# Joined 512-column products in the MLP, earlier weight splits for the latents, and gated outputs transposed in three parts

## What is computed

```python
# first_block, layer 0: moba and fox heads; layer 1: differential and sliding-window (swa) heads
y = concat([ya * silu(ga), yb * silu(gb)]);   x = x + y @ w_out_ab
...
y = concat([yc * silu(gc), yd * silu(gd)]);   x = x + y @ w_out_cd
# second_block, per layer i: a mixer (latent attention "mla", then stick-breaking), cross attention, MLP
lat = h @ w_dkv
c_q  = rmsnorm_2(lat[..., :384], g_q)
c_kv = rmsnorm_2(lat[..., 384:640], g_kv)
k_pe = lat[..., 640:]
q = c_q @ w_uq;  kv = c_kv @ w_ukv           # per head: 192 and 256 columns
...
h = h + mem_cross_attn(...)
h = h + square(relu(rmsnorm_2(h) @ w_in)) @ w_out      # w_in: 1024 x 4096
```

## Time and profile before

| | |
|---|---|
| median of 3 runs | 1026.99 us (1026.68 to 1027.73) |
| the profiled execution's own time | 1027.6 us |
| its span in the trace | 1025.8 us |
| PE busy | 989.2 us (96% of the span) |
| DVE busy | 627.6 us (61%) |
| ACT busy | 548.2 us (53%) |
| mean granted clock of PE | 0.985 of full speed |

### The profile page before, as it was taken

The page is one execution under the profiler, slowest core; times in us unless marked ns, Lnnn a source line. Parts: engine busy times, 40 slices in busy tenths (PEclk is TensorE's granted clock), DMA queues, the critical chain, the costliest instruction groups (busy, mean ns, idle before and its releaser), DMA issues.

```text
span 1025.8 us, 15748 instructions
## 1 busy us (share of the span) xinstructions
PE 989.2 (96%) x6172; PEld 879.7 (86%) x6172; DVE 627.6 (61%) x1208; ACT 548.2 (53%) x1029; POOL 38.3 (4%) x83
## 2 busy tenths in 40 slices
PE   8899999999999979999999999999999999999997
PEld 7677778787787979887999999899988889999995
DVE  5867545486864476656765555557873658455554
ACT  6575564366684445545744434455673557444352
POOL 4011000001130000000000000000000000000000
PEclk9899989999999989999999999999999999999999
DMA  9776312565332434343556565666435435565551
GB/s 288 218 164 124 124 41 88 163 202 164 123 114 62 122 90 150 124 128 121 182 186 200 173 201 176 235 164 177 152 103 185 146 104 195 176 203 171 198 186 42
DMA packets 114167, 158.14 MB, mean 154 GB/s; under 512 B 13783, under 2 KB 55085, under 8 KB 114093
## 3 DMA queue, kind: packets, MB, share of 16 engines
q1 hardware_dynamic: 113656, 156.56, 49.4%
q10 hardware_dynamic: 436, 0.56, 0.2%
HBM read 156.06 MB, written 1.05 MB: 153 GB/s over the span
## 4 chain that ended last, share of the span: by engine, by line
PE 84%; DVE 6%; ACT 4%; issue 2%; SPq 1%; DMA 1%; DVEq 0%; ACTq 0%
PE bank L475 24%; PE bank L476 24%; PE bank L477 24%; PE bank L613 3%; DVE w_lo L1771 2%; PE bank L638 2%; PE bank L627 2%; PE bank L607 1%; PE bank L529 1%; DMA raw<-in_w_in_ab 1%; ACT xT_hi L1319 1%; SPq L2472 1%; DVE xT_lo L1828 1%; ACT pb L1438 1%; PE bank L592 1%
## 5 line engine op out<-in xcount | busy, mean ns | idle before, releaser
L1771 DVE TENSOR_TENSOR w_lo<-raw,w_hi 128x1024 fp32r<-128x1024 f32 (+2 forms) x292 | 336.2, 1195 | 179.2 <-ACT w_hi L1274 178.9
L1274 ACT CAST w_hi<-raw 128x1024 fp32r<-128x1024 f32 (+2 forms) x292 | 283.4, 1027 | 146.6 <-DMA raw<-in_mlp_w_in 74.2
L475 PE MATMUL bank<-xT_hi,w_hi 128*128 128x256 f32 x784 | 224.5, 286 | 3.0 <-DVE xT_lo L1828 2.0
L476 PE MATMUL bank<-xT_lo,w_hi 128*128 128x256 f32 x784 | 222.5, 284 | 0.0
L477 PE MATMUL bank<-xT_hi,w_lo 128*128 128x256 f32 x784 | 222.5, 284 | 0.0
L475 PE MATMUL bank<-w_hi,xT_hi 128*128 128x512 f32 (+1 forms) x432 | 161.8, 375 | 9.0 <-issue 4.0
L477 PE MATMUL bank<-w_hi,xT_lo 128*128 128x512 f32 (+1 forms) x432 | 157.9, 365 | 0.0
L476 PE MATMUL bank<-w_lo,xT_hi 128*128 128x512 f32 (+1 forms) x432 | 157.8, 365 | 0.0
L475 PEld LDWEIGHTS bank<-xT_hi,w_hi 128*128 128x128 f32 x784 | 151.0, 193 | 4.9 <-issue 3.1
L476 PEld LDWEIGHTS bank<-xT_lo,w_hi 128*128 128x128 f32 x784 | 151.0, 193 | 0.7
L477 PEld LDWEIGHTS bank<-xT_hi,w_lo 128*128 128x128 f32 x784 | 151.1, 193 | 0.0
(11 more groups left out here) (243 smaller groups left out, 1096.8 us busy)
## 6 DMA issues: line engine op xcount, KB each, us to landing
raw<-in_mlp_w_in SPq DMA_DIRECT2D x32, 1024.0 KB, 5.4
raw<-in_mlp_w_out SPq DMA_DIRECT2D x32, 1024.0 KB, 5.1
raw<-in_w_in_ab SPq DMA_DIRECT2D x13, 1024.0 KB, 9.3
raw<-in_w_in_cd SPq DMA_DIRECT2D x13, 1024.0 KB, 5.1
raw<-in_xa_w_kv SPq DMA_DIRECT2D x8, 1024.0 KB, 5.2
raw<-in_sb_w_qkv SPq DMA_DIRECT2D x16, 512.0 KB, 5.1
raw<-in_w_out_ab SPq DMA_DIRECT2D x4, 1024.0 KB, 5.2
raw<-in_w_out_cd SPq DMA_DIRECT2D x4, 1024.0 KB, 5.2
```

The costliest lines, as they stand in the source:

```text
L475: pe.matmul(o, wh, ih, start=start, stop=False, skip_group_check=True)
L476: pe.matmul(o, wh, il, start=False, stop=False, skip_group_check=True)
L1274: nc.scalar.copy(w_hi[:, u % SLOTS, a], raw[:, u % SLOTS, a]).then_inc(hi_ready, 1)
L1771: V.tensor_tensor(w_lo[:, u % SLOTS, a], raw[:, u % SLOTS, a], w_hi[:, u % SLOTS, a].bitcast(F32), ALU.subtract).then_inc(lo_ready, 1)
```

## The change

**Joined products.** `xT_hi` and `xT_lo` become the two halves of one array `xT`, so that hi and lo of a chunk lie side by side. In the MLP's blocks 2 to 7 of both layers `up` multiplies `w_hi` once by all 512 columns [hi | lo] into a whole bank, and `w_lo` by the 256 columns of hi into the bank's left half. Each chunk f now has a bank of its own, so one block fills all of banks 4 to 7. The sum of the bank's halves is formed outside PE: ACT copies the right half to the arena, DVE adds the left half, and one DVE instruction does relu and square together. `relu_ready` now means that DVE has added, and PE waits for it chunk by chunk before it writes the next block.

**Early splits.** In `part` and `rope_keys` the first half waits for the first half of the unit only. On ACT and DVE the split of uh0 moves ahead of the first latents' `hi` and `lo`, that of uh1 ahead of the query latents', and only uh2's is left ahead of the inverse root; the row copy is placed behind dq1's split, and DVE's `lo` of the query latents behind its work on the rotary key.

**Three parts.** The transposes of the gated outputs of fox and swa heads are split: chunks 4 and 5 (`GATE_PARTS` entry 0, heads 0 to 3) and chunk 6 (heads 4 and 5) go into the last steps of the pipeline, chunk 7 stays behind it.

```diff
-        xT_hi = sb("xT_hi", [P, KC, S], F32R)
-        xT_lo = sb("xT_lo", [P, KC, S], F32R)
+        xT = sb("xT", [P, KC, 2, S], F32R)
+        xT_hi, xT_lo = xT[:, :, 0, :], xT[:, :, 1, :]
...
+        GATE_PARTS = ((0, 2, 4, 3), (2, 1, 5, 5), (3, 1, 6, 7))
...
             def part(key, u, b, first, token_layout, r, only=(0, 1)):
 
+                take(u, 0 if first else 1)
                 if first:
-                    take(u)
                     begin(key, b)
...
-            def gated(name, panel, b0, need):
-
-                return transposes(name, lambda t, c: arena[:, panel, t * PANEL + c * P:t * PANEL + (c + 1) * P],
-                                  4, lambda t: (y_ready, need), b0)
+            def gated(name, panel, b0, need, first=0, chunks=4):
+
+                return transposes(name, lambda t, c: arena[:, panel, t * PANEL + (first + c) * P:t * PANEL + (first + c + 1) * P],
+                                  chunks, lambda t: (y_ready, need), b0)
 
             yr = {}
 
             def gate(key, *a):
                 yr[key] = gated(key, *a)
+
+            def gate_part(key, panel, n, ks):
+
+                first, chunks, b0, last = GATE_PARTS[n]
+                yr[key, n] = gated((key, n), panel, b0, ks[last]["output"], first, chunks)
+
+            def gate_chunk(key):
+
+                def ready(k):
+                    n, c = ((0, 0), (0, 1), (1, 0), (2, 0))[k - 4]
+                    return yr[key, n](c)
+                return ready
 
...
                 12: [lambda: memory(0)], 13: [lambda: gate("yab0", 3, 0, heads_of("moba")[-1]["output"])],
-                14: [mem_part(0)], 15: [mem_part(1)], 17: [half("oab", 0, 0, X, "yab0")], 18: [half("oab", 0, 1, X, "yab0")]})
-            gate("yab1", 7, 4, heads_of("fox")[-1]["output"])
+                14: [mem_part(0)], 15: [mem_part(1)], 16: [lambda: gate_part("yab1", 7, 0, heads_of("fox"))],
+                17: [half("oab", 0, 0, X, "yab0"), lambda: gate_part("yab1", 7, 1, heads_of("fox"))], 18: [half("oab", 0, 1, X, "yab0")]})
+            gate_part("yab1", 7, 2, heads_of("fox"))
             for n in range(2):
-                project_half("oab", 1, n, X, lambda k: yr["yab1"](k - 4), (lambda: turn_x(("n", 1), 0, 6)) if n else None)
+                project_half("oab", 1, n, X, gate_chunk("yab1"), (lambda: turn_x(("n", 1), 0, 6)) if n else None)
...
             def rope_keys(first):
                 u = names["dp", 0]
+                take(u, 0 if first else 1)
                 if first:
-                    take(u)
                     begin("dp", 3)
...
-                def up(odd, u, blk):
-                    pe.wait_ge(relu_ready, relu0 + 2 * (blk - 2) + 2)
+                def up(u, blk):
+
                     for n in range(2):
-                        up_half(odd, n, u + n)
+                        take(u + n)
+                        for f in range(4):
+                            b = 4 + f
+                            if n == 0:
+                                pe.wait_ge(relu_ready, relu0 + 4 * (blk - 2) + f + 1)
+                            for c in range(4):
+                                k = 4 * n + c
+                                wh, wl = (flat(w, u + n)[:, c * BLK + f * P:c * BLK + (f + 1) * P] for w in (w_hi, w_lo))
+                                pe.matmul(banks[b][:, :], wh, xT[:, k].rearrange("p a s -> p (a s)"), start=k == 0, stop=False, skip_group_check=True)
+                                ins = pe.matmul(banks[b][:, 0:S], wl, xT_hi[:, k, :], start=False, stop=k == KC - 1, skip_group_check=True)
+                            if n == 1 and f < 3:
+                                ins.then_inc(written[b], 1)
+                        ins.then_inc(units_used, 1)
...
-            x_turned(("x", 0), U["ocd", 1, 1], U["dq", 0], True)
...
+            x_turned(("x", 0), U["ocd", 1, 1], U["dq", 0])
+            row_copy(("x", 0))
+            used(U["dk", 0])
...
             latent(2)
+            used(U["dp", 0])
             latent(0)
             latent(1)
-            used(U["dk", 0])
-            used(U["dp", 0])
             used(U["dq", 1])
...
                     splits(u + 6 if blk else u + 5)
-                    for p in range(2):
+                    for p in range(2 if blk < 2 else 0):
                         b = 4 + 2 * odd + p
                         if p == 0:
-                            act.wait_ge(written[b], mlp_base[i][b] + blk // 2 + 1)
+                            act.wait_ge(written[b], mlp_base[i][b] + 1)
                         else:
                             act.wait_ge(units_used, max(u + 2, u0 + 3))
                         nc.scalar.activation(pan(4, p), banks[b][:, :], ACT.Relu).then_inc(relu_ready, 1)
+                    for f in range(4 if blk >= 2 else 0):
+                        if f < 3:
+                            act.wait_ge(written[4 + f], mlp_base[i][4 + f] + blk - f % 2)
+                        else:
+                            act.wait_ge(units_used, u + 2)
+                        nc.scalar.copy(pan(4, f // 2)[:, f % 2 * S:(f % 2 + 1) * S], banks[4 + f][:, S:2 * S]).then_inc(second_ready, 1)
...
             x_turned(("x", 0), "ocd", U["ocd", 1, 1], U["dq", 0])
-            for n, c, chunks in ((2, 3, 2), (0, 0, 2), (1, 2, 1)):
+            used(U["dk", 0])
+
+            def latent(n, c, chunks):
+
                 ps = condition(dve, ("lat", n))
                 dve.wait_ge(hiT_ready, lo_T[0] + chunks)
                 for k in range(chunks):
                     lo(hT_lo[:, c + k, :], ps[:, k * S:(k + 1) * S], hT_hi[:, c + k, :], evac_gain(("lat", n), k))
+
+            latent(2, 3, 2)
             dve.wait_ge(row_ready, row_no["x", 0])
             own.sig(V.tensor_tensor(row_sq, row[:, :], row[:, :], ALU.mult))
             link(V.tensor_tensor(row_rope, rope[:, :], row[:, :], ALU.mult))
...
             for n, (r0, c0) in enumerate([(0, 0), (64, 64), (0, 64), (64, 0)]):
                 ins = V.tensor_copy(halves[r0:r0 + 64, c0:c0 + 64], ident[r0:r0 + 64, r0:r0 + 64])
                 own.sig(ins, roped if n == 3 else None)
+            used(U["dp", 0])
+            latent(0, 0, 2)
+            latent(1, 2, 1)
...
-            used(U["dk", 0])
-            used(U["dp", 0])
...
                     for p in range(2):
-                        dve.wait_ge(relu_ready, h0 + 2 * blk + p + 1)
                         if p == 0 and (blk > 0 or i > 0):
                             dve.wait_ge(hT_ready, h0 + 2 * blk)
-                        V.tensor_tensor(pan(5, p), pan(4, p), pan(4, p), ALU.mult).then_inc(h_ready, 1)
+                        if blk < 2:
+                            dve.wait_ge(relu_ready, relu0 + 2 * blk + p + 1)
+                            V.tensor_tensor(pan(5, p), pan(4, p), pan(4, p), ALU.mult).then_inc(h_ready, 1)
+                            continue
+                        for f in (2 * p, 2 * p + 1):
+                            o = pan(4, p)[:, f % 2 * S:(f % 2 + 1) * S]
+                            dve.wait_ge(second_ready, second0 + 4 * (blk - 2) + f + 1)
+                            V.tensor_tensor(o, banks[4 + f][:, 0:S], o, ALU.add).then_inc(relu_ready, 1)
+                            own.last = (relu_ready, relu0 + 4 * (blk - 1) + f + 1)
+                        own.settle()
+                        V.scalar_tensor_tensor(out=pan(5, p), in0=pan(4, p), scalar=0.0, in1=pan(4, p), op0=ALU.max, op1=ALU.mult).then_inc(h_ready, 1)
+                        own.last = (h_ready, h0 + 2 * blk + p + 1)
                     for p in range(2):
                         dve.wait_ge(hhi_ready, h0 + 2 * blk + p + 1)
                         V.tensor_tensor(hb[1][:, 2 * odd + p, :], pan(5, p), hb[0][:, 2 * odd + p, :].bitcast(F32),
```

41 lines of the change are left out of this document (24 added, 17 removed).

## The result

| | before | changed |
|---|---|---|
| median | 1027.36 us (1026.68 to 1027.79, 4 runs) | 1016.02 us (1015.21 to 1019.75, 4 runs) |
| the profiled execution's own time, and its span | 1027.6, 1025.8 us | 1015.2, 1013.4 us |

The ratio is 0.9897, with a 95% interval of 0.9872 to 0.9922: 11.3 us less, between 8.0 and 13.2. The forecast was 1013.9 us, 13.1 us less. Timed again together with the last experiments (`e11_change_again`), the same kernel took 1015.14 us against 1026.7 (ratio 0.989, 0.9869 to 0.991), 11.6 less.

The account below looks back on a forecast made before the run. PE, busy for 96% of the span, was taken to bound the kernel. Terms of 4.8, 5.1 and 3.2 us sum to 13.1 us less, a median of 1013.9 us, range 1011.0 to 1018.8.

Parts of the forecast that it names:

- Joined products, 4.8 us: MLP up blocks: 384 groups of three matmuls become pairs, 12.5 ns less each; bounds 0 and 7.2 us.
- 227.3 + 119.9 = 347.2 ns: MLP up blocks: a joined pair costs one 512-column plus one 256-column matmul, against 359.7 ns for three.
- Early splits, 5.1 us: Latents: 0.6 from the rotary keys' wait, 3.1 from idle before mla_head(0), 1.4 from the slow clock behind it.
- The margin of the inverse root: Latents: DVE's inverse-root chain ends about 367.7, PE reaches value_scales at 370.8, so 3 us of margin remain.
- the unchanged wait of 2.72 us: Behind value_scales: PE's wait on a chain through DVE moves with it, its 2.72 us unchanged.
- Three parts, 3.2 us: Gated outputs of fox and swa heads: splitting the transposes wins 1.75 + 1.4 us; bounds 0 and 2 x 2.0.
- DVE, which evacuates values behind chunk 5, may add 0.1: Swa heads' end: DVE's evacuation of values behind chunk 5 may cost 0.1 us of the gain there.
- The latents in part: Rival, latents: hT_lo ends at 363 instead of 361, idle and perhaps the slow stretch return; 2.7 us less, 1016.6; chance 0.14.
- PE waiting for the additions: Slower rival, MLP up blocks: PE waits for DVE's additions because evacuation must fit into a down block; chance 0.03.
- The pair without gain: Rival, MLP up blocks: the joined pair costs what the three did; 8.3 us saved in all, 1018.7; chance 0.11.
- The second slow stretch: Rival: the slow clock behind the 2.72 us wait goes too, worth 1.4 us, giving 1012.5; chance 0.10.
- The rival of the late additions: Slower case, up(3) to up(7), both layers: 1.3 us of waiting for DVE's additions gives 1029.5; chance 0.03.

Follow-up runs that it names:

- e11_change_again: The changed kernel itself, unaltered, timed again on the same chip as the last experiments: 1015.14 us.
- e7: Changed kernel with sixteen long then sixteen short matmuls per weight unit, and DVE's swa low part of chunks 4 and 5 one step later: 1012.08 us.
- e4: Changed kernel with each chunk's four long matmuls in an up block placed together, then its four short ones: 1014.84 us.
- e5: Changed kernel with each joined 512-column matmul done as two of 256; banks, copies and additions kept: 1021.1 us in one execution.
- e6: Changed kernel with w_lo also multiplied by all 512 columns, adding a lo*lo product: 1053.57 us in one execution.
- e2: Kernel before the change with the early splits alone, separate products and gates as before: 1020.59 us.
- e9: Changed kernel with sixteen long then sixteen short matmuls, later swa low part, and unread matmuls filling the wait before the first mla scores: 1012.11 us.

## Why the prediction was right, and where its sizes were off

- **What bounds the kernel** was read rightly: each gain came out of PE's stream or out of a place where PE stood still, and DVE's and ACT's added work cost nothing.
- **Joined products, 4.8 us: the mis-sized term.** The change brings 2.5 us (1.1 and 1.4 by the two layers); by blocks, 12 x (0.22 - 0.03) = 2.3, and the rest is the wait of 0.26 us ahead of MLP 1. The step that failed is "227.3 + 119.9 = 347.2 ns", taken "because both members have their own rows": each was measured in a stream of its own kind, and a stream that alternates costs 352.8 ns. e7 shows that the sum holds where like stands with like (347 ns), and e4 and e7 that the order alone makes the difference; e5 excludes the banks and additions, e6 a dearer long matmul. By the Trainium skill's 2.5 ns for a warm matmul (TensorE: Matmul & The Clock Gate, "Wait — 56ns, not 53.3ns?") the part would bring an estimated 1.0 us in any order; e5 against e7 (11.51 and 11.10 us) shows 12.8 ns for each matmul taken away, so the trace does not agree.
- **Early splits, 5.1 us:** 0.60 (forecast 0.6) and 4.85 (forecast 3.1 + 1.4), in e2 5.46 together. `mla_head(0)` followed `lat_ss` at once: from start to start 2.05 us, before 5.46, so 3.41 us were won where the printed wait of 3.07 had been counted. It took 357.02 to 361.36 = 4.34 us, which is the forecast 1.4. The margin of the inverse root, 2.9 us, and the unchanged wait of 2.72 us came as written.
- **Three parts, 3.2 us:** 2.6. Fox 1.78 (1.75), swa 0.84 (1.4). The step that was too small is "DVE, which evacuates values behind chunk 5, may add 0.1": it cost 0.73, by what e7 wins when it moves this work one step later. DVE not only does 0.76 us of work there, but stands waiting for ACT's cast with the values behind it.
- **Rivals.** The latents in part: no. PE waiting for the additions: no. The pair without gain: half true, with 12.5 ns a pair forecast and 6.9 measured. The second slow stretch stayed, as the forecast had it. The rival of the late additions never arose, and its sum was off: only up(3) to up(7) wait for additions, 10 blocks in two layers and not 12, so 1.3 us of waiting would give some 1027 and not 1029.5 us.
- The terms sum to 10.6 us and the median fell by 11.3 (11.6 when timed again), within the interval. The 12.4 us of the profiled span hold 1.8 of luck with the clock: had the profile been the only measure, the mis-sized term would have been half covered.

## What to carry to other kernels

Price a matmul by its start-to-start distance, but in a stream of the mix that you will build: a price from a uniform stream holds for runs of like matmuls, so put the long ones together and the short ones together. When work is moved into an engine's order ahead of something that another engine waits for, count the wait that comes with it and not only its duration. Compare two traces by the distance between the same two instructions on both sides of an edit; the difference of the spans carries slow stretches that no edit made.

## What was not expected of the hardware

- Alternating a 512-column with a 256-column matmul costs 352.8 ns a pair, four and four 350, sixteen and sixteen 347; an all-long stream has 226.7 ns each. The down block behind an alternating up block is 0.03 us longer as well, and is not behind sixteen short ones. Why the change of length costs is not shown.
- Slow stretches of the granted clock (0.50, some 3.5 us, 1.7 us lost each) come in all profiles, though PE is busy for 96% of the span, in places that partly change from one execution to the next, and they hide waits: in e7 the fox values at 138.58 wait 1.66 us, in e9, where three stretches in a row began ahead of them, not at all. The one at the first mla scores is tied to its wait of 2.72 us: nine of ten profiles with the wait open, none of three with it filled. The one in the latents' heads went with its wait of 3.07 us (three of three profiles with it, none of ten without). At a wait of 1.77 us near 740 (752 before) one came in six of thirteen profiles, always within 1.5 us of the wait's end.
